# State products around the heads' turn, the normaliser as a column of the value products, and output weights loaded in parts

## What is computed

```python
s = einsum('nhtd,nhsd->nhts', qc, kc) * exp(dmat - mt[..., None])
num = w_inter[..., None] * einsum('nhtd,nhde->nhte', qc, C) + einsum('nhts,nhse->nhte', s, vc)
den = w_inter * einsum('nhtd,nhd->nht', qc, n) + sum(s, axis=-1)
h = num / maximum(abs(den), exp(-mt))[..., None]
C_new = w_old[..., None, None] * C + einsum('nhsd,nhse->nhde', kw, vc)
n_new = w_old[..., None] * n + sum(kw, axis=2)
...
hn = rmsnorm(og * hc, hnorm_g).reshape(N, T, A_INNER)
out = ((hn + skip * xconv) * silu(z)) @ w_out
return x + gate * out, (C, n, m, new_conv)
```

## Time and profile before

| | us |
|---|---|
| median of 3 runs | 2092.03 (2087.93 to 2093.74) |
| the profiled execution | 2096.07 |
| its span in the trace | 2094.4 |
| PE busy | 1932.2 (92% of the span) |
| DVE busy | 702.7 |
| ACT busy | 473.6 |
| POOL busy | 228.1 |

### The profile page before, as it was taken

The page is one execution under the profiler, slowest core; times in us unless marked ns, Lnnn a source line. Parts: engine busy times, 40 slices in busy tenths (PEclk is TensorE's granted clock), DMA queues, the critical chain, the costliest instruction groups (busy, mean ns, idle before and its releaser), DMA issues. The chain is left out here.

```text
span 2094.4 us, 26021 instructions
## 1 busy us (share of the span) xinstructions
PE 1932.2 (92%) x9695; PEld 1156.0 (55%) x9695; DVE 702.7 (34%) x1555; ACT 473.6 (23%) x1032; POOL 228.1 (11%) x333
## 2 busy tenths in 40 slices
PE   5779999999999999997899999779889999999878
PEld 3345646554655466446773447745555555555457
DVE  3113232423242332230112125057662444444332
ACT  1311211211121112110002011236452333333210
POOL 0000100010001000100000000025352212111000
PEclk9769999999999999998999999879899999999989
DMA  9931551344136323623221226510015344443431
GB/s 302 387 144 68 203 212 43 142 167 175 55 129 214 127 83 141 231 93 156 81 80 40 70 51 222 156 75 1 1 40 209 149 185 172 188 181 140 130 94 43
DMA packets 119292, 281.79 MB, mean 135 GB/s; under 512 B 33224, under 2 KB 41870, under 8 KB 115447
## 3 DMA queue, kind: packets, MB, share of 16 engines
q1 hardware_dynamic: 101004, 170.57, 24.4%
q0 software_dynamic: 12928, 109.54, 13.0%
q10 hardware_dynamic: 5268, 0.36, 0.2%
HBM read 227.79 MB, written 60.86 MB: 138 GB/s over the span
## 5 line engine op out<-in xcount | busy, mean ns | idle before, releaser
L2173 PE MATMUL sample_bank<-area 128*128 128x508 f32 x512 | 234.3, 600 | 4.8 <-DVE area L2414 4.8
L1074 DVE SCALAR_TENSOR_TENSOR mlstm_cring<-mlstm_cring,mlstm_cur_old,mlstm_bank 128x512 f32<-128x512 f32 x128 | 87.1, 743 | 223.4 <-PE mlstm_bank L840 223.4
L2173 PEld LDWEIGHTS sample_bank<-area 128*128 128x128 f32 x512 | 92.0, 190 | 106.6 <-issue 98.7
L1354 PE MATMUL proj_bank<-stage,area 128*128 128x512 f32 x320 | 142.5, 604 | 6.3 <-ACT area L1431 6.3
L758 PE MATMUL mlstm_bank<-h,stage 128*128 128x272 f32 x512 | 122.7, 403 | 10.9 <-DVE mlstm_xconv L1134 6.4
L813 PE MATMUL mlstm_bank<-h,stage 128*128 128x272 f32 x512 | 121.2, 395 | 0.0
L758 PEld LDWEIGHTS mlstm_bank<-h,stage 128*128 128x128 f32 x512 | 99.7, 195 | 32.7 <-issue 7.4
L824 PE MATMUL mlstm_bank<-stage,h 128*128 128x512 f32 x256 | 114.1, 599 | 0.0
L813 PEld LDWEIGHTS mlstm_bank<-h,stage 128*128 128x128 f32 x512 | 96.0, 190 | 27.9 <-issue 9.1
L775 PE MATMUL mlstm_bank<-stage,h 128*128 128x512 f32 x256 | 110.9, 594 | 0.0
L1354 PEld LDWEIGHTS proj_bank<-stage,area 128*128 128x128 f32 x320 | 60.9, 193 | 87.6 <-issue 86.1
(11 more groups left out here) (512 smaller groups left out, 2708.1 us busy)
## 6 DMA issues: line engine op xcount, KB each, us to landing
stage<-in_a_w_in SPq DMA_DIRECT2D x16, 2048.0 KB, 8.7
mlstm_cring<-in_state_C SPq DMA_DIRECT2D x32, 1024.0 KB, 5.5
o_Cs<-mlstm_cring POOLq DMA_DIRECT2D x32, 1024.0 KB, 4.7
stage<-in_a_ada_w SPq DMA_DIRECT2D x4, 2048.0 KB, 12.5
stage<-in_a_w_out SPq DMA_DIRECT2D x4, 2048.0 KB, 11.6
sample_winr<-in_cache_kv_win SPq DMA_DIRECT2D x8, 1024.0 KB, 5.3
o_win_s<-in_cache_kv_win SPq DMA_DIRECT2D x1, 8128.0 KB
stage<-in_w_kv SPq DMA_DIRECT2D x3, 2048.0 KB, 7.8
```

The source lines that it names most:

```text
L1074: dve.scalar_tensor_tensor(c, c, cur_old[:, n:n + 1], bank[:, b_big("outer", n * KH + k), :], ALU.mult, ALU.add).then_inc(E["c_new"], 1)
L1354: last = pe.matmul(o, h[:, k, a * P:(a + 1) * P], w[:, k, :], start=(k == 0), stop=(k == KD - 1))
L2173: t = pe.matmul(out, S.w1[:, c, o * 8 + k, :], xt[:, k, :, o:o + M - 1], start=(k == 0 and o == 0), stop=(k == 7 and o == 1))
```

## The change

- The values are stored as two halves of 256 columns, and each has one more column behind it (`HV`); that column is set to one once, at the phase's start.
- The ten products with the column of ones (L882), their semaphore and the DVE wait for them go. In their place the value product of the first half takes 257 columns, so that the row sum is its last column. A num tile is now two products (257 and 256 columns) in two banks, 20 in all.
- DVE makes the reciprocal for each tile apart, four small operations for each of four tiles, and scales a tile in two halves.
- Of the four state products two stay ahead of the heads' turn and two go behind it, and with them the normaliser state n. On DVE the part for n goes to the end of the head. The rotation of banks follows: the next head's first two big products wait for the last two hn tiles, and PE waits at a head's end until ACT has copied all four state products.
- In phase_project the weights of the second pass are loaded in four parts of 4 groups `k` each, and a part is started as soon as the first pass is through its groups; the second pass waits for part after part in its first block.

```diff
+        HV = AD // 2
...
-        v = sb("v", [P, TT, AD]); vs = sb("vs", [P, AD])
+        v = sb("v", [P, TT, 2, HV + 1]); vs = sb("vs", [P, AD])
...
-               + [(E["st_ok"], 4, i) for i in range(4)] + [(E["num_ok"], 4, i) for i in range(4)]
-               + [(E["cp_ok"], 4, i) for i in range(4)] + [(E["hn_used"], 4, i) for i in range(4)])
-        AT = {"xc": 0, "v": 4, "q": 8, "k": 12, "kw": 16, "outer": 20, "s": 52, "num": 56, "cp": 60, "hn": 64}
+               + [(E["st_ok"], 4, i) for i in range(4)] + [(E["num_ok"], 8, i) for i in range(8)]
+               + [(E["cp_ok"], 4, 0), (E["cp_ok"], 4, 1)] + [(E["hn_used"], 4, 4 + i) for i in range(4)]
+               + [(E["cp_ok"], 4, 2), (E["cp_ok"], 4, 3)])
+        AT = {"xc": 0, "v": 4, "q": 8, "k": 12, "kw": 16, "outer": 20, "s": 52, "num": 56, "cp": 64, "hn": 66}
...
-                    p = AT[kind] + i
+                    p = AT[kind] + i + (4 if kind == "cp" and i >= 2 else 0)
                     if p >= 4:
                         s, n, at = big[p - 4]
                         pe.wait_ge(s, h * n + at + 1)
-                    else:
-                        pe.wait_ge(E["hn_used"], h * 4 + p + 1)
+                    elif p < 2:
+                        pe.wait_ge(E["hn_used"], h * 4 + p + 3)
                     return bank[:, p % 4, :]
...
+                    second = take_big("num", 2 * a + 1) if a > 1 else bank[:, b_big("num", 2 * a + 1), :]
+                    first = bank[:, b_big("num", 2 * a), :]
                     for s in range(a + 1):
                         w = st[:, XE[s] + (a - s) * P:XE[s] + (a - s + 1) * P]
-                        last = pe.matmul(bank[:, 7, a:a + 1], w, C("ones")[:, 0:1], start=(s == 0), stop=(s == a))
-                last.then_inc(E["den_mm"], 1)
-                for a in range(TT):
-                    o = take_big("num", a)
-                    for s in range(a + 1):
-                        w = st[:, XE[s] + (a - s) * P:XE[s] + (a - s + 1) * P]
-                        last = pe.matmul(o, w, v[:, s, :], start=(s == 0), stop=(s == a))
+                        pe.matmul(first[:, 0:HV + 1], w, v[:, s, 0, :], start=(s == 0), stop=(s == a))
+                        last = pe.matmul(second[:, 0:HV], w, v[:, s, 1, 0:HV], start=(s == 0), stop=(s == a))
                     last.then_inc(E["num_mm"], 1)
 
                 pe.wait_ge(E["kw_ok"], h * 5 + 5)
-                for i in range(KH):
+                def state(i):
                     o = take_big("cp", i)
                     for a in range(TT):
-                        last = pe.matmul(o, kw[:, a, i * P:(i + 1) * P], v[:, a, :], start=(a == 0), stop=(a == TT - 1))
+                        last = pe.matmul(o, kw[:, a, i * P:(i + 1) * P], v[:, a, :, 0:HV], start=(a == 0), stop=(a == TT - 1))
                     last.then_inc(E["cp_mm"], 1)
-                o = take_small("n")
-                for a in range(TT):
-                    pe.matmul(o[0:9, :], C("one9"), kw[:, a, :], start=(a == 0), stop=False)
-                for k in range(KH):
-                    last = pe.matmul(o[0:9, k * P:(k + 1) * P], C("seq_of9")[:, k, :], kwd[:, :], start=False,
-                                     stop=(k == KH - 1))
-                last.then_inc(E["n_mm"], 1)
-
+
+                state(0)
+                state(1)
...
                 pe.wait_ge(E["hn_ok"], h + 1)
                 for i in range(KH):
                     o = take_big("hn", i)
...
+                state(2)
+                state(3)
+                o = take_small("n")
+                for a in range(TT):
+                    pe.matmul(o[0:9, :], C("one9"), kw[:, a, :], start=(a == 0), stop=False)
+                for k in range(KH):
+                    last = pe.matmul(o[0:9, k * P:(k + 1) * P], C("seq_of9")[:, k, :], kwd[:, :], start=False,
+                                     stop=(k == KH - 1))
+                last.then_inc(E["n_mm"], 1)
+                pe.wait_ge(E["cp_ok"], h * 4 + 4)
...
+            dve.memset(v[:, :, :, HV:HV + 1], 1.0)
...
-                    dve.tensor_copy(v[:, i, :], bank[:, b_big("v", i), :]).then_inc(E["v_ok"], 1)
+                    dve.tensor_copy(v[:, i, :, 0:HV], bank[:, b_big("v", i), :].rearrange("p (j x) -> p j x", j=2)).then_inc(E["v_ok"], 1)
...
-                dve.wait_ge(E["den_mm"], h + 1)
...
-                dve.tensor_scalar(den[:, 0:TT], bank[:, 7, 0:TT], -1.0, None, ALU.mult)
-                dve.drain()
-                dve.tensor_tensor(den[:, 0:TT], bank[:, 7, 0:TT], den[:, 0:TT], ALU.max)
-                dve.drain()
-                dve.tensor_tensor(den[:, 0:TT], den[:, 0:TT], cur[:, 2, 0:TT], ALU.max)
-                dve.drain()
-                dve.reciprocal(den[:, 0:TT], den[:, 0:TT])
-                dve.drain()
                 for a in range(TT):
                     dve.wait_ge(E["num_mm"], h * 4 + a + 1)
-                    dve.scalar_tensor_tensor(og[:, a, :], bank[:, b_big("num", a), :], den[:, a:a + 1], og[:, a, :],
-                                             ALU.mult, ALU.mult).then_inc(E["num_ok"], 1)
+                    norm, d = bank[:, b_big("num", 2 * a), HV:HV + 1], den[:, a:a + 1]
+                    dve.tensor_scalar(d, norm, -1.0, None, ALU.mult)
+                    dve.drain()
+                    dve.tensor_tensor(d, norm, d, ALU.max)
+                    dve.drain()
+                    dve.tensor_tensor(d, d, cur[:, 2, a:a + 1], ALU.max)
+                    dve.drain()
+                    dve.reciprocal(d, d)
+                    dve.drain()
+                    for j in range(2):
+                        part = og[:, a, j * HV:(j + 1) * HV]
+                        dve.scalar_tensor_tensor(part, bank[:, b_big("num", 2 * a + j), 0:HV], d, part,
+                                                 ALU.mult, ALU.mult).then_inc(E["num_ok"], 1)
...
-                dve.wait_ge(E["n_mm"], h + 1)
-                n_h = S.n0[:, bass.ds(h * AD, AD)]
-                dve.tensor_copy(S.w_cur[:, :], S.w_old9[:, bass.ds(h, 1)])
-                dve.drain()
-                dve.scalar_tensor_tensor(n_h, n_h, S.w_cur[:, 0:1], bank[0:9, b_small("n"), :], ALU.mult,
-                                         ALU.add).then_inc(E["n_ok"], 1)
...
                 dve.tensor_tensor(szt[:, :, :], xconv[:, :, :], szt[:, :, :], ALU.mult).then_inc(E["act_ok"], 1)
+
+                dve.wait_ge(E["n_mm"], h + 1)
+                n_h = S.n0[:, bass.ds(h * AD, AD)]
+                dve.tensor_copy(S.w_cur[:, :], S.w_old9[:, bass.ds(h, 1)])
+                dve.drain()
+                dve.scalar_tensor_tensor(n_h, n_h, S.w_cur[:, 0:1], bank[0:9, b_small("n"), :], ALU.mult,
+                                         ALU.add).then_inc(E["n_ok"], 1)
...
-            for s in range(2):
-                sp.wait_ge(E["wo_mm"], 2 * (s + 1))
-                sp.dma_start(slot_k16[s], wo[:, :, 512 + s * 256:768 + s * 256]).then_inc(w_in[s], 16)
+            for k in range(4):
+                sp.wait_ge(*((E["wo_head"], k + 1) if k < 3 else (E["wo_mm"], 4)))
+                for s in range(2):
+                    sp.dma_start(slot_k16[s][:, k * KH:(k + 1) * KH, :],
+                                 wo[:, k * KH:(k + 1) * KH, 512 + s * 256:768 + s * 256]).then_inc(wo_in[k], 16)
...
+                    elif k % KH == KH - 1 and b == 3:
+                        last.then_inc(E["wo_head"], 1)
             for s in range(2):
-                pe.wait_ge(w_in[s], 32)
                 for j in range(2):
                     b = 2 * s + j
                     pe.wait_ge(E["x_new"], b + 1)
                     for o, at in ((bank[:, b, :], 0), (bank[:, 4 + b, :], HALF)):
                         for k in range(16):
+                            if s == 0 and j == 0 and at == 0 and k % KH == 0:
+                                pe.wait_ge(wo_in[k // KH], 32)
```

More of the change, by code:

```diff
@@ L617, in phase_mlstm @@
                + [(E["kw_ok"], 5, 1 + i) for i in range(4)] + [(E["c_new"], 32, i) for i in range(32)]
[L618 to L620 removed]
+               + [(E["st_ok"], 4, i) for i in range(4)] + [(E["num_ok"], 8, i) for i in range(8)]
+               + [(E["cp_ok"], 4, 0), (E["cp_ok"], 4, 1)] + [(E["hn_used"], 4, 4 + i) for i in range(4)]
+               + [(E["cp_ok"], 4, 2), (E["cp_ok"], 4, 3)])
+        AT = {"xc": 0, "v": 4, "q": 8, "k": 12, "kw": 16, "outer": 20, "s": 52, "num": 56, "cp": 64, "hn": 66}
         small = ([(E["xc_ok"], 4, i) for i in range(4)] + [(E["vs_ok"], 1, 0), (E["v_ok"], 5, 4), (E["convst_ok"], 1, 0), (E["qs_ok"], 1, 0),
                  (E["kw_ok"], 5, 0)] + [(E["z_ok"], PAIR, i) for i in range(PAIR)] + [(E["os_ok"], 1, 0)]
[L623 removed]
+                 + [(E["o_ok"], 5, i) for i in range(5)] + [(E["sts_ok"], 1, 1), (E["hns_used"], 1, 1), (E["n_ok"], 1, 1)])
         SMALL = {"xc": 0, "vs": 4, "vfold": 5, "conv": 6, "qks": 7, "kwd": 8, "z": 9, "os": 9 + PAIR, "o": 10 + PAIR,
[L625 removed]
+                 "ss": 15 + PAIR, "hns": 16 + PAIR, "n": 17 + PAIR}
```

(7 more changed lines are left out.)

6 lines of the change are left out of this document (1 added, 5 removed).

## The result

| | before | after |
|---|---|---|
| median, runs of one chip, us | 2092.89 (2087.93 to 2095.73, 4 runs) | 2078.79 (2076.84 to 2081.56, 4 runs) |
| ratio, 95% interval | | 0.9929 (0.9909 to 0.9948) |
| the profiled execution / its span | 2096.07 / 2094.4 | 2076.84 / 2075.2 |

The change makes the kernel 14.1 us faster by the medians, less than half of the 32.8 us of the prediction, and the time lies 3.8 us above the range.

A forecast was written before the change was run, and what follows sets the result against it. PE, busy for 92% of the span, was taken as the bound. Gains of 18.2 us (loop), 5.7 (between the phases) and 8.9 (output weights) sum to 32.8, giving 2059.2 from the median, stated as 2060; range 2049 to 2075.

The forecast's parts named there:

- the next head starts at once: Head's end: PE goes on without idle time, 11.3 us of products covering DVE's L1134; 2.18 us gained a turn.
- The prediction's own condition: Sign at the heads' turn: the forecast is wrong if PE waits there for over 2 us.
- The tail of a head: From the samples' products to the next head: 35.36 us become 30.7, from ones, clock and turn, less two new waits.
- The wait at the turn: Ahead of a head's first transpose: PE newly waits 0.6 us for DVE and ACT, with two state products as cover.
- Between the phases: PE's idle time between loop and output passes falls from 17.88 to 12.2 us, 5.7 us gained.
- The output weights: Second output pass, weights loaded in parts: its 6.19 us wait and 3.0 us of low clock go, 8.9 us gained.
- Each turn lowers the clock: Rival, heads' turn: idle time and transposes amid products lower the clock four times, 6.8 us in all, 2067; 13%.
- The value products keep the low clock: Rival, value products: the low clock comes from the small sample products, not the ones; 6.9 us, 2067; 8%.
- DVE's halves cost as wholes: Rival, DVE's scaling: half tiles take as long as wholes, 0.7 us more at each new wait, 5.6 in all, 2066; 8%.
- Nothing gained outside the loop: Rival, between phases and second output pass: other waits remain, so the 5.7 and 8.9 us are not gained; 2074; 5%.
- Strided values are slower: Rival, products reading `v`: PE reads rows of 257 columns slower; at half the pace +90 us, 2150; 4%.
- the forecast sum: Loop over the heads: tails, turns and the last head's end together gain 18.2 us.

The follow-up runs named there:

- p4: The kernel before with only PE's loop over the four heads written out, so PE has no jump: 2090.56 us, ratio 0.9982.
- p6: The kernel before with the new state stored in four parts, each as soon as ACT has copied it: 2093.39 us, ratio 0.9997.
- e1: The changed kernel with the result's store first and only one of 128 partitions of the new state stored (output incomplete): 2064.42 us, one run.
- e6: The changed kernel with the result's store ahead of the state's and one extra 1.1 MB store a head behind them: 2079.35 us, ratio 0.9931.
- p2: The kernel before with only the normaliser as a column and the value products in halves: 2082.22 us, ratio 0.9942.
- e5: The changed kernel with POOL's two stores swapped, the result's ahead of the new state's, nothing left out: 2063.78 us, ratio 0.9855.
- p1: The kernel before with only the second output pass's weights loaded in parts: 2085.29 us, ratio 0.9956.
- e3: The changed kernel with PE's loop over the four heads written out, stores as they were: 2063.20 us, ratio 0.9849.
- e4: The changed kernel with PE's loop written out and the state stored in four parts, the result's store between: 2059.13 us, ratio 0.9836.
- e2: The changed kernel with the state stored in four parts, each when copied, the result's store between second and third: 2065.36 us, ratio 0.9855.
- p3: The kernel before with only the new order, two state products and n behind the heads' turn: 2095.54 us, ratio 1.0016.

## Why the prediction was wrong, point by point

**The step that failed** is "and the next head starts at once". Two things were wrong in it. The turn's 2.18 us was read as a wait for DVE's L1134, and so seen to be covered by 11.3 us of products; p4, p6 and the packets show that it was the jump's own. That half did no harm: in after only 0.41 us of it is left. The other half did: POOL's two stores were costed for the barrier behind the loop, at the last head, but not at the three turns, where the new order puts them right beside PE's jump. There the second block of instructions waits until they are nearly through, 10.5 us over the three turns, and the low clock behind the stops takes 6.1 more. The prediction's own condition, that PE waits for over 2 us at the turn, is what happened; its rivals had no instruction load among them.

The Trainium skill (Runtime: NRT & Kernel Launch, Instruction fetch mechanics) says that a taken branch to a page outside the window forces a DMA fetch before execution goes on, and that crossing from one block of 16 KiB to the next is mostly hidden. The runs agree with the first (the stops of before go with the jump in p4) and with the size (1.13 MB in 69 packets). With the second they agree in e1, and in after not: 3.25 to 3.80 us a turn.

The first block comes nearly in time in after because its packet passes at 333.4, ahead of the stores' first packets (334.2) and with 2.6 us of work left. Why it is asked for so early there is argued, not shown: it follows the end of ACT's last copy, which gives the last `cp_ok`, by 1.2 us (332.2), as it does in e1 and e6 by 1.2 and 1.3. What sets that moment in before stays open; the last semaphore there, `hn_ok`, had come at about 326.2, 13 us ahead of the packet.

**The tail of a head.** The value products start at 304.74 and run at 1.00, where before had 0.61 in their first part; they take 9.52 us to the state products with a new wait of 0.47 (forecast 9.6, with 0.8). The wait at the turn is 0.90 in head 0 and 0.57 in the others (forecast 0.6). Up to the next head's first row it is 31.66 us where 30.7 was forecast; 0.41 of the difference is the first block. This part of the sum was right to about a microsecond, and p2 measured 11.0 us for what was 12.6 in it.

**Between the phases**: 5.1 us for 5.7. With the result's store earlier (e5) the idle time is 11.12 us and not 12.76, so that the stores cost some 1.6 us of it. **The output weights**: p1 measured 7.9 us for 8.9, and the second pass starts without a wait. In the two traces the passes gain 10.7; of the 1.8 us that go beyond, 1.4 are of the first pass, from L1323's start to L1337's 60.41 us where 61.83 were, and it was not in the sum. Its first 10 us have a granted clock of 0.83 in after and 0.70 before.

**The rivals.** *Each turn lowers the clock*: a low clock at every turn did come, but behind the stops and not behind the transposes, behind which the state products run at 1.00 (324.40 to 331.60). The Trainium skill (TensorE: Matmul & The Clock Gate, Part 4: PE-mode transpose) says that transposes don't count as work for the clock in the same way, which spoke for this rival; the 1.00 behind them at all four heads gives it no support here. *The value products keep the low clock*: no, 1.00. *DVE's halves cost as wholes*: no, the third tile's wait was 0.47 and not 1.5. *Nothing gained outside the loop*: no. *Strided values are slower*: no, the 16 instructions of two state products take 7.04 us, where 16 of before take 7.03.

With the stop away the forecast sum is there: in e3's trace the loop lasts 779.7 us, 17.1 less than before, where 18.2 was forecast. That e4, with 2059.1 us, is the predicted number to a microsecond is partly luck, since e4 also removes the 0.4 us of the first block and has the stores earlier for the barrier.

## What to carry to other kernels

At each jump of this loop PE had to get its next blocks of instructions, and stores of 1 MB issued near that point held the second one up; keep a jump clear of large stores, by storing earlier or in parts, or write the loop out for the engine that bounds the kernel. Idle time at a loop's end that goes on after the named releaser is done, and idle time marked "issue" some instructions behind the jump, are signs of it. When work is moved, look also at what its followers on the DMA queues now stand beside.

## What was not expected of the hardware

- A jump back costs PE about 2.1 us of idle time in the kernel before, which covers little of it (6.4 us over three turns, gone in p4), whether or not a store is under way (p6: 6.5). From the block's packet to PE's next product 2.7 to 3.2 us pass at the first turn of seven runs.
- The block behind it, asked for some 3 us later, came up to 3.8 us late where two stores of 1 MB were on the way, and 0.3 to 0.5 us late or not at all where they were through (e5, e2, e1).
- The trace put an idle time at a jump down to the last semaphore event: the 2.18 us of the earlier trace rows bore the name of DVE's L1134, although the one that PE needed was over 0.43 us before that idle time began.
- Wide products behind the one-column products had a granted clock below 1 in before, p3 and p4 (0.61 in the stretch of the earlier trace rows, 0.84 in p3's and 0.83 in p4's first 10 us), and 1.00 in after and p2, which don't have them.
